# Reordering the start of a two-block fp32 kernel: tokens and value projection first, the other turns later, convolution ahead of queries and keys

## The reference

```
proj = x @ w_in[l]                                  # x: 256 x 1024, w_in[l]: 1024 x 8192
q, k, v, cb, cc, cu, qm, gates = split(proj)        # 1024, 1024, 1024, 512, 512, 512, 512, 3 x 1024
q = rope(q, cos, sin); k = rope(k, cos, sin)        # cos, sin from the positions
y_attn = diff_attention(q, k, v, lam, ...)
y_conv = cb * causal_conv3(cc * cu, conv_w[l])
y_mem  = memory_attention(qm, mem, w_mem_kv[l])
g = sigmoid(gates)
merged = g0 * (y_attn @ w_br_attn) + g1 * (y_conv @ w_br_conv) + g2 * (y_mem @ w_br_mem)
x = layer_norm(ALPHA * x + merged @ w_out[l])       # then 16 experts, 2 per token, and a second layer_norm
```

## Time and profile before

| | before |
|---|---|
| device time, median of 3 runs | 2620.08 us (2618.93 to 2621.36) |
| profiled execution, its own time | 2617.45 us |
| span of its trace | 2615.4 us |
| PE busy | 2438.9 us (93%) |
| DVE, ACT busy | 671.5 us (26%), 435.8 us (17%) |
| first product of the first layer starts | 37.06 us |
[...]

### The profile page before, as it was taken

One profiled execution on the slowest core, in us unless ns is written; L12 is line 12 of the kernel. 1 busy time (PEld: TensorE's weight loads), 2 busy tenths in 40 slices (PEclk: granted clock), 3 DMA queues, 4 the chain that ended last, 5 costly groups with the idle time before them and its releaser, 6 DMA issues.

```text
span 2615.4 us, 24868 instructions
## 1 busy us (share of the span) xinstructions
PE 2438.9 (93%) x10391; PEld 1552.3 (59%) x10391; DVE 671.5 (26%) x1572; ACT 435.8 (17%) x960; POOL 4.2 (0%) x27
## 2 busy tenths in 40 slices
PE   5999989899979999898999699889999998999998
PEld 4686758644456877486444345534444443668887
DVE  3310262311134102633111346420101002551101
ACT  1011240211110111402111224320000001241001
POOL 0000000000000000000000000000000000000000
PEclk8999989899989999898999899999999999999999
DMA  7444553399953445631999611011101312202330
GB/s 282 161 151 193 203 226 129 114 418 427 428 236 146 161 163 203 277 129 69 417 428 427 281 46 52 1 65 64 64 32 70 139 65 96 96 34 97 126 148 17
DMA packets 34780, 449.86 MB, mean 172 GB/s; under 512 B 5112, under 2 KB 5994, under 8 KB 7274
## 3 DMA queue, kind: packets, MB, share of 16 engines
q1 hardware_dynamic: 32208, 447.63, 42.8%
q10 hardware_dynamic: 2458, 0.59, 0.1%
HBM read 447.15 MB, written 1.05 MB: 171 GB/s over the span
## 4 chain that ended last, share of the span: by engine, by line
PE 81%; DMA 8%; DVE 5%; ACT 2%; issue 2%; DVEq 1%; ACTq 0%; SPq 0%
PE banks L440 80%; DMA ring<-in_w_exp_up 8%; DVE arena L1433 1%; DVE tiny L1794 1%; PE banks L984 1%; PE banks L526 1%; DVE arena L1811 0%; ACT arena L1273 0%; DVE X L1825 0%; PE banks L751 0%; ACT arena L1119 0%; DVE tiny L1382 0%; DVE arena L1404 0%; ACT X L1148 0%; ACTq L1077 0%
## 5 line engine op out<-in xcount | busy, mean ns | idle before, releaser
L440 PE MATMUL banks<-arena,ring 128*128 128x256 f32 (+1 forms) x3520 | 1086.3, 470 | 37.1 <-ACT arena L1273 25.5
L440 PEld LDWEIGHTS banks<-arena,ring 128*128 128x128 f32 x3520 | 670.7, 191 | 446.6 <-issue 376.1
L440 PE MATMUL banks<-X,ring 128*128 128x256 f32 x1792 | 392.4, 382 | 16.6 <-DVEq L1551 11.5
L440 PEld LDWEIGHTS banks<-X,ring 128*128 128x128 f32 x1792 | 342.7, 191 | 67.7 <-issue 20.8
L440 PE MATMUL banks<-ring,arena 128*64 128x512 f32 x1536 | 335.8, 594 | 8.1 <-DMA ring<-in_w_exp_up 6.8
L440 PE MATMUL banks<-arena 128*128 128x128 f32 (+5 forms) x1712 | 260.8, 344 | 6.9 <-issue 2.4
L440 PEld LDWEIGHTS banks<-ring,arena 128*64 128x64 f32 x1536 | 112.1, 137 | 218.4 <-issue 214.6
L440 PEld LDWEIGHTS banks<-arena 128*128 128x128 f32 (+2 forms) x1712 | 187.6, 185 | 52.6 <-issue 36.7
L1101 ACT ACTIVATE arena<-banks 128x256 f32<-128x256 f32 (+1 forms) x132 | 59.6, 455 | 593.3 <-PE banks L440 584.3
L1825 DVE SCALAR_TENSOR_TENSOR X<-banks,ada,X 128x256 f32<-128x256 f32 x48 | 21.8, 481 | 308.5 <-PE banks L440 306.9
L440 PE MATMUL banks<-arena,mean_d 128*128 128x256 f32 (+1 forms) x208 | 69.6, 467 | 26.9 <-issue 10.9
(11 more groups left out here) (199 smaller groups left out, 1251.7 us busy)
## 6 DMA issues: line engine op xcount, KB each, us to landing
ring<-in_w_in SPq DMA_DIRECT2D x38, 2048.0 KB, 8.8
ring<-in_w_exp_gate SPq DMA_DIRECT2D x32, 2048.0 KB, 13.5
ring<-in_w_exp_up SPq DMA_DIRECT2D x32, 2048.0 KB, 16.6
ring<-in_w_exp_down SPq DMA_DIRECT2D x32, 2048.0 KB, 11.5
ring<-in_w_ada SPq DMA_DIRECT2D x24, 2048.0 KB, 8.2
ring<-in_w_gate SPq DMA_DIRECT2D x10, 2048.0 KB, 8.0
ring<-in_w_up SPq DMA_DIRECT2D x10, 2048.0 KB, 8.0
ring<-in_w_out SPq DMA_DIRECT2D x8, 2048.0 KB, 14.1
```

Of the source, the lines that this page charges most:

```text
L440: ins = nc.tensor.matmul(out, weights, moving, start=start, stop=stop)
```

## The change

SP issues only x first, then the weights without waiting for the parameters; mem and ctx_2 go between the second and the third tile. PE turns x alone and starts with the two value tiles. In the first layer it turns the parameters, mem and ctx_2 behind them. Then come the convolution inputs, two gates and the branch product, and only then queries and keys. ACT's part of the parameter work (exponential, sigmoid, two sines) stands between its copies of `cbT` and of `ccT`. The arena's temporary places move so that x, mem and ctx_2 outlive the values. In the second layer the value product takes over the chunk by chunk wait for the normalised tokens (`normed`). POOL makes `ident` first.

```
-            for n in ("x", "mem", "ctx_2"):
-                sp.dma_start(raw[n], a[n].rearrange("(c p) d -> p c d", p=P)).then_inc(s_inputs, 16)
+            def load(n):
+                sp.dma_start(raw[n], a[n].rearrange("(c p) d -> p c d", p=P)).then_inc(s_input[n], 16)
+
+            load("x")
             sp.sem_inc(s_free, RING)
-
-            sp.wait_ge(s_params, PARAM_DMAS * 16)
...
-                for c in (0, 1, 2, 3, 4, 5, 6, 7, 8, 12, 13):
+                for c in (4, 5, 6, 7, 8, 12, 13):
                     tile(block_of("w_in", l * 16 + c))
+                    if l == 0 and c == 5:
+                        load("mem")
+                        load("ctx_2")
                 tile(block_of("w_br_conv", l))
+                for c in (0, 1, 2, 3):
+                    tile(block_of("w_in", l * 16 + c))
...
+                        if normed and tc == 0:
+                            pe.wait_ge(s_norm, C.next("norm"))
...
-            pe.wait_ge(s_consts, 1)
-            pe.wait_ge(s_ones, 1)
-            pe.wait_ge(s_inputs, 48)
-            pe.wait_ge(s_params, PARAM_DMAS * 16)
-            for n in ("x", "mem", "ctx_2"):
+            def turned_input(n):
+                pe.wait_ge(s_input[n], 16)
                 for c in range(0, DC, 2):
                     b = ring_bank("act")
...
-            b = ring_bank("dve")
-            nc.tensor.transpose(bank[b][:, 0:104], stackA[0:104, :], ident[0:104, 0:104])
-            nc.tensor.transpose(bank[b][:, 128:224], stackB[0:96, :], ident[0:96, 0:96])
-            full(nc.tensor.transpose(bank[b][:, 256:302], stackC[0:46, :], ident[0:46, 0:46]), b, "dve")
-            ring_bank("dve")
-            all_read()
-            pe.wait_ge(s_cond, 1)
-            pe.wait_ge(s_tables, 1)
+                return s_read["act"], C.value("read_act")
+
+            def turned_params():
+                pe.wait_ge(s_consts, 2)
+                pe.wait_ge(s_params, PARAM_DMAS * 16)
+                b = ring_bank("dve")
...
+            pe.wait_ge(s_consts, 1)
+            pe.wait_ge(s_ones, 1)
+            turned_input("x")
 
             for l in range(DEPTH):
                 all_read()
-                tile_features(X, T, "dve", normed=(l > 0))
-                for t in range(3):
-                    tile_features(X, T, "dve")
+                token_product(X, normed=(l > 0))
                 token_product(X)
-                token_product(X)
+                if l == 0:
+                    turned_params()
+                    mem_turned = turned_input("mem")
+                    turned_input("ctx_2")
                 tile_features(X, T, "act")
                 tile_features(X, T, "act")
                 tile_features(X, T, "dve")
...
                 tile_features(cbT, T, "dve", kc=CC, width=D)
+                for t in range(4):
+                    tile_features(X, T, "dve")
+                if l == 0:
+                    release()
+                    pe.wait_ge(*mem_turned)
+                    pe.wait_ge(s_cond, 1)
                 tile_features(memT, T, "act")
...
+                for c in range(CC):
+                    copy_chunk(cbT[:, c, :])
+                if l == 0:
+                    act.wait_ge(s_lam, 1)
+                    fn(lamsum, lamsum, ACT.Exp).then_inc(s_lam_exp, 1)
+
+                    fn(tiny[:, 16:32], tiny[:, 0:16], ACT.Sigmoid).then_inc(s_lam_exp, 1)
+                    act.wait_ge(s_angle, 1)
+                    fn(cosT[:], ang[:, 1, :], ACT.Sin).then_inc(s_angle, 1)
+                    fn(sinT[:], ang[:, 0, :], ACT.Sin).then_inc(s_angle, 1)
+                for c in range(CC):
+                    copy_chunk(ccT[:, c, :])
```

More of the change, by code:

```diff
@@ L106, in sem @@
             return ctx.enter_context(nc.semaphore(name))
-        s_inputs = sem("inputs_loaded")
+        s_input = {n: sem(n + "_loaded") for n in ("x", "mem", "ctx_2")}
         s_params = sem("params_loaded")
@@ L199, in view @@
             return v
[L202 to L207, removed]
+        raw = {"x": view(0, TC, D), "mem": view(2048, TC, D), "ctx_2": view(14344, TC, D)}
+        stackA, stackB, stackC = (view(11272 + P * i, P) for i in range(3))
+        lamrows = view(11656, 4, DEPTH, 64)
+        lamsum = view(12168, 4)
+        pos_i = view(12228, T).bitcast(I32)
+        ang = view(12484, 6, T)
         qT, kT = view(0, HEADS, T), view(2048, HEADS, T)
@@ L364, in _ @@
             g = nc.gpsimd
-            for m, v in ((ident, 0.0), (before, 1.0), (causal, 0.0), (behind, 0.0), (mean_h, 1.0 / 64)):
+            g.memset(ident[:], 0.0)
+            g.drain()
+            g.affine_select(out=ident[:], in_=ident[:], compare_op=ALU.not_equal, fill=1.0, base=0,
+                            pattern=[[-1, P]], channel_multiplier=1).then_inc(s_consts, 1)
+            for m, v in ((before, 1.0), (causal, 0.0), (behind, 0.0), (mean_h, 1.0 / 64)):
                 g.memset(m[:], v)
@@ L508, in tile_features, with token_product @@
                 used()
-            def token_product(src):
+            def token_product(src, normed=False):
                 s = next_tile()
@@ L753, in _ @@
                     full(ins, b, "act")
-            b = ring_bank("dve")
-            nc.tensor.transpose(bank[b][:, 0:104], stackA[0:104, :], ident[0:104, 0:104])
-            nc.tensor.transpose(bank[b][:, 128:224], stackB[0:96, :], ident[0:96, 0:96])
-            full(nc.tensor.transpose(bank[b][:, 256:302], stackC[0:46, :], ident[0:46, 0:46]), b, "dve")
-            ring_bank("dve")
-            all_read()
-            pe.wait_ge(s_cond, 1)
-            pe.wait_ge(s_tables, 1)
+                return s_read["act"], C.value("read_act")
[3 more added lines that the diff above has]
+                b = ring_bank("dve")
+                nc.tensor.transpose(bank[b][:, 0:104], stackA[0:104, :], ident[0:104, 0:104])
+                nc.tensor.transpose(bank[b][:, 128:224], stackB[0:96, :], ident[0:96, 0:96])
+                full(nc.tensor.transpose(bank[b][:, 256:302], stackC[0:46, :], ident[0:46, 0:46]), b, "dve")
+                ring_bank("dve")
+            pe.wait_ge(s_consts, 1)
+            pe.wait_ge(s_ones, 1)
+            turned_input("x")
             for l in range(DEPTH):
                 all_read()
-                tile_features(X, T, "dve", normed=(l > 0))
-                for t in range(3):
-                    tile_features(X, T, "dve")
+                token_product(X, normed=(l > 0))
                 token_product(X)
-                token_product(X)
+                if l == 0:
+                    turned_params()
+                    mem_turned = turned_input("mem")
+                    turned_input("ctx_2")
                 tile_features(X, T, "act")
@@ L1189, in expert_pairs, with copy_input @@
                         done(nc.scalar.copy(yex[:, 512 * nh:512 * nh + 512], bank[5 + nh][:]))
-            for dst, t0 in ((X, 0), (memT, 0), (X, T)):
+            def copy_input(dst, t0):
                 for c in range(0, DC, 2):
                     done(nc.scalar.copy(dst[:, c:c + 2, t0:t0 + T], take()[:].rearrange("p (c t) -> p c t", c=2)))
[L1195 to L1201, removed]
+            copy_input(X, 0)
             for l in range(DEPTH):
@@ L1206, in _ @@
                         copy_chunk(vtok[:, tc, 512 * half:512 * half + 512], 512)
-                for dst in (cbT, ccT):
-                    for c in range(CC):
-                        copy_chunk(dst[:, c, :])
+                if l == 0:
+                    copy_input(memT, 0)
+                    copy_input(X, T)
+                for c in range(CC):
+                    copy_chunk(cbT[:, c, :])
+                if l == 0:
+                    act.wait_ge(s_lam, 1)
[6 more added lines that the diff above has]
+                    copy_chunk(ccT[:, c, :])
                 act.drain().then_inc(s_gate_copied, 1)
@@ L1550, in _ @@
                 tsc(sinT[32 * q:32 * q + 32, :], sinT[32 * q:32 * q + 32, :], -1.0, None, ALU.mult)
-            drain().then_inc(s_tables, 1)
+            drain()
             for l in range(DEPTH):
[L1555 to L1564, removed]
                 v.memset(zT[:, :, 0:TAPS - 1], 0.0)
@@ L1584, in _ @@
                 drain().then_inc(s_gates_used, 1)
+                for dst, scale in ((qT, 0.125), (kT, 1.0)):
+                    for h in range(HEADS):
+                        b = take()
+                        stt(tmp1, b[:, 0:T], scale, cosT[:], ALU.mult, ALU.mult)
+                        for q in range(4):
+                            i, o = slice(32 * q, 32 * q + 32), slice(32 * (q ^ 1), 32 * (q ^ 1) + 32)
+                            ins = stt(tmp2[o], b[i, 0:T], scale, sinT[i], ALU.mult, ALU.mult)
+                        drain()
+                        done(tt(dst[:, h, :], tmp1, tmp2, ALU.add))
+                        drain()
                 def conditioning(t):
```

3 lines of the change are left out of this document (removed).

## The result

The changed kernel is slower. Its time is 2638.11 us (median of 4 runs, 2637.77 to 2639.04), against 2620.72 us for the kernel before in the same session (4 runs, 2618.93 to 2621.44): a ratio of 1.0071, 95% interval 1.0058 to 1.0083. The forecast was 2611.4 us, with 2619 as the upper end of its range. The time lies nearest to the rival in which ACT is held in its issues (2633 us).

A forecast was written before the change was run, and what follows sets the result against it. PE, busy 93% of the span, was taken as the bound, so only its idle time at the start could be won: -20.1 + 1.0 + 0.3 + 6.0 + 3.0 + 0.9 + 0.2 = -8.7 us, giving 2611.4 us, range 2607.5 to 2619.

The forecast's parts named there:

- the rival in which ACT is held in its issues: At the start, a full ACT queue holds its last issue to 35 us; +12.9 us, 2633 us, chance 0.12.
- The new start of the first product: First layer: ACT's copies of x start at 13.45 us, the first product at 17.0 instead of 37.06; 20.1 us won.
- the first of the signs: Listed as showing the prediction wrong: at the start, ACT's issues reaching far beyond 12 us.
- nothing in the trace shows a limit: Argument against ACT being held at the start: no limit on its queue's outstanding packets was seen in the earlier trace.
- Turns behind the values: Stack transposes and bank fills of mem and ctx_2, moved behind the value tiles, uncovered on PE; 6.0 us lost.
- The slower fills of x: If the clock falls in the parameter wait, later fills take x's 0.89 us instead of 0.66; 0.3 us counted.
- ACT's gap: PE waits in front of the third ccT chunk for ACT's parameter work between cbT and ccT; 3.0 us lost.
- Its clock: PE's clock may fall after the wait between cbT and ccT; 0.9 us lost, bounds 0 and 2.1.
- Parameters, 1.0 us: After the value tiles, PE waits for parameters landing at 47.6 us; 1.0 us lost, bounds 0 and 3.
- Clock at the first product: The first chunk of the first product loses 2.1 us to a low clock, both before and after the change.
- What I counted at nothing: Queries and keys behind the branch, s_conv, the third convolution input and the second layer's start: 0 us, at best -0.5.
- Is time at the start kept to the end?: Each us won at the start counted once, with no factor, since a shift moves the expert stage as a whole.

The follow-up runs named there:

- e4: The changed kernel with the router's weights moved from third-last to last of ACT's transfers; 2613.78 us, ratio 0.9981 to the kernel before.
- e2: The changed kernel with both router transfers issued behind ACT's copies of ctx_2, on a semaphore of their own; 2612.64 us, ratio 0.9977 to the kernel before.
- e10: The kernel before without SP's wait for the parameters, and with the router's weights as ACT's last transfer; 2645.14 us, ratio 1.0103 to the kernel before.
- e5: e4 with exponential and sigmoid moved ahead of the four cbT copies, the sines staying between cbT and ccT; 2610.13 us, ratio 0.9960 to the kernel before.
- e6: e5 with x copied by DVE instead of ACT, and SP waiting for the parameters behind the two value tiles; 2598.54 us, ratio 0.9918 to the kernel before.
- e3: The kernel before with only SP's wait for the parameters taken out; 2648.80 us, ratio 1.0113 to the kernel before.
- e1: The changed kernel with SP waiting for all parameters behind x, ahead of the first weight tile; 2617.48 us, ratio 0.9995 to the kernel before.
- e9: The changed kernel with SP waiting for the parameters behind the two value tiles, ahead of mem and ctx_2; 2614.82 us, ratio 0.9981 to the kernel before.

## Why the prediction was wrong

**The step that failed** is in "The new start of the first product": "ACT still has its 25 issues and a table load ahead, which end at 12.17 + 1.28 = 13.45 us". I took that duration from a run in which SP had only the three inputs on its queue, 816 packets that were through by 11.8 us, and carried it into one in which SP's queue has work until 44 us. It ended at 40.89: ACT's issues reached far beyond 12 us, the first of the signs that the prediction had named for being wrong. The first product was to win 20.1 us and lost 7.2; these 27.3 us are more than the whole error of 26.7 between forecast and median.

The mechanism was in the text as a rival with a chance of 0.12 and a price of 2633 us: ACT held until some 35 us. It was right in kind and in sign. Its weighing failed: "nothing in the trace shows a limit" was true of the trace and no evidence, since in that trace SP's queue was all but empty (812 of 816) when ACT issued behind the router's weights.

That its time came so near (35 us against 39.0, 2633 against 2638.1) is in part luck, since two errors cancel. It supposed that 1650 outstanding packets, some 103 a transfer engine, are bearable; in the changed kernel the issue came free only with 1304 served and 1154 to come, some 72 an engine. And it had the small packets served at 26 a us from 5.3 us on, while 1272 (1304 less the 32 of the earlier trace rows) in 33.7 us are 38 a us, since mem and ctx_2 stand in SP's queue with smaller packets (from 30 us on, when they were through, it was 27). With 1304 served, the count at which the issue came free, and its own rate it would have had the hold end at 54 us (5.3 + 1272 / 26).

**Turns behind the values, 6.0 us:** measured 6.0. The slower fills of x (0.89 us), which the prediction put down to the clock, stood in the kernel before beside a granted clock of 1.00 from 16 to 20 us, so that step was the author's estimate.

**ACT's gap, 3.0 us:** 2.6, in the predicted place and with the predicted releaser. **Its clock, 0.9** with bounds 0 and 2.1: the upper bound came, in each of the kernels that had the gap (e4: 0.72 of the full clock at 78 to 82 us, behind a gap of 2.59).

**Parameters, 1.0 us:** none in the changed kernel, as PE was too late to wait; 2.46 in e2 and none in e4, where the values end at about 49.9. So they land near 50 and not at 47.6. One for one held, with 16 KB packets also: 604 to 601 in e10.

**Clock at the first product, 2.1 us on both sides:** by the same reading 2.25 before, 2.55 in the changed kernel and 3.1 in e4 (10.0 us for a chunk). Off by 0.3 to 0.9.

**What I counted at nothing** was nothing: queries and keys behind the branch, the third convolution input (behind ACT's gap PE waits for no other engine until attention), and the second layer's start. There ACT's eight chunks took 4.04 us as before, and PE's products followed, at a granted clock of 0.50 from 780 to 784 us (before: 0.58 from 764 to 768). Timeline of the changed kernel:

```profile
779.83 4.04 ACT L1166 ACTIVATE X<-arena,vecA 128x256 f32<-128x256 f32 x8 [2.32 <-DVE arena L1473]
780.58 19.74 PE L446 MATMUL banks<-ring,X 128*128 128x512 f32 x39 [4.03 <-ACT X L1166]
```

**Is time at the start kept to the end?** Yes, about one for one. Attention's first matmul moved by +18.6, -5.4, -9.9 and -21.1 us (changed kernel, e4, e5, e6), the medians by +17.4, -5.5, -9.8 and -21.4. Within one trace the shift moves by some 2 us: in the changed kernel it was +18.6 at attention, +16.3 at the second layer's first product (780.58 against 764.29) and +20.4 at the end.

**Open.** What exactly holds the issue is not settled. Seen: where weights come right behind x, the issue behind `sinks` is held to 12.6 to 13.5 us; where mem and ctx_2 with their 4 KB packets come first (e3, e10), it isn't, and there twice as many of ACT's packets had been served when it began (366 and 369, against 183 in the changed kernel). The issue behind the router's weights is held to 39.0 and 39.8 us, in both kinds. With SP's queue empty none was held (e1: the last three took 0.34 to 0.46 us), and a held one was released when that queue ran empty (e9: at 15.72 us, 560 packets served).

The counts at the release fit, roughly, a limit on ACT's packets still to come (those of issues not yet made counted in) that holds only while SP's queue has work: 1174 of 1416 at the end of the short hold in e2, 1154 of 2458 at the end of the long one in the changed kernel, 1297 in e3. How much work SP has seems not to matter: in the changed kernel 1180 of its 1680 packets were left at the end of the short hold and 120 at the end of the long one. With SP's queue empty or nearly so, 1859 (before, at 11.31 us) were no bar, and in e9 the held issue was released with 1915 to come. No run was made to test such a limit. Whether something of the queue runs short, and what, no run here tells.

## What to carry to other kernels

An engine that issues transfers and also computes has its computation behind its issues (ACT's table load stood at 39.61 us instead of 12.17); before bulk loads are started earlier, look at who still has small transfers to issue, and put the one with the most packets last (e4: some 24 us below the changed kernel) or let an engine without issues do the first work (e6: some 40 us below it). A duration read from the trace holds only for what else was going on then: an issue of 0.46 us beside a queue with 4 packets left took 25.55 beside one with 1180. And parameters beside an early stream of 16 KB packets came through one packet for one (604 to 601 in e10), so count their packets, not their bytes.

## What the runs showed of the hardware

- One instruction that issues a 64-byte transfer occupied ACT for 25.55 us (28.75 in e3, 0.46 in the kernel before). Here the issue itself was the cost.
- Small packets (604, of 0.5 KB on average) and those of a queue of 16 KB packets (601) were served one for one over 22 us (e10).
- A gap of 2.6 us of PE was followed by a stretch at 0.57 of the full clock (0.50 from 104 to 106 us) and cost another 2.1 us, so that removing a wait of 2.6 us gave 4.5 at attention (e5 against e4). A gap of 2.93 us elsewhere left the clock at 1.00, so the length of a gap alone doesn't tell.
